# Splitting slot 0's rows and planning the slots before the slot tables, in a fused encoder layer on one core

## The reference

```python
t = rms_norm(h, norm_moe_g).reshape(B * S, D)                 # 1024 rows of 1024
g_prob = softmax(t @ w_group + b_group); g_idx = argmax(g_prob) # 4 groups
e_logits = (t @ w_router + b_router)[group g_idx]             # 4 experts in a group
top_p, top_i = top_k(softmax(e_logits), 2)                    # two experts per row
weights = g_w * top_p / sum(top_p)
for e in range(16):
    he = silu(t @ w_gate[e]) * (t @ w_up[e])                  # 1024 -> 512
    moe = moe + gates[:, e:e + 1] * (he @ w_down[e])          # 512 -> 1024
h = h + moe
```

## Time and profile before

| | us |
|---|---|
| median of 3 runs | 1494.66 |
| their range | 1491.63 to 1494.96 |
| the profiled execution | 1493.72 |
| its span, first to last instruction | 1491.9 |
| PE busy | 1413.1 (95%) |
| DVE busy | 972.7 (65%) |
| ACT busy | 855.9 (57%) |
| POOL busy | 147.1 (10%) |

### The profile page before, as it was taken

One profiled execution on the slowest core, in us unless ns is written; L12 is line 12 of the kernel. 1 busy time (PEld: TensorE's weight loads), 2 busy tenths in 40 slices (PEclk: granted clock), 3 DMA queues, 4 the chain that ended last, 5 costly groups with the idle time before them and its releaser, 6 DMA issues.

```text
span 1491.9 us, 21096 instructions
## 1 busy us (share of the span) xinstructions
PE 1413.1 (95%) x7429; PEld 1082.8 (73%) x7429; DVE 972.7 (65%) x1763; ACT 855.9 (57%) x1553; POOL 147.1 (10%) x205
## 2 busy tenths in 40 slices
PE   6999999999999989999999999988999999999996
PEld 5888989544445544458878888767788888888885
DVE  5513116367658866767763343378888888989887
ACT  6321457366657656653252333344677887888776
POOL 1000000122300200000000000001111112221221
PEclk9999999999999999999999999997999999999998
DMA  6331134420020001021120001146996666666694
GB/s 226 71 111 35 61 107 155 177 103 1 1 113 1 1 7 51 29 95 47 43 113 29 29 29 57 51 148 247 352 361 201 213 216 211 216 216 217 222 373 133
DMA packets 89396, 189.01 MB, mean 127 GB/s; under 512 B 14313, under 2 KB 24553, under 8 KB 88562
## 3 DMA queue, kind: packets, MB, share of 16 engines
q1 hardware_dynamic: 80050, 166.11, 31.2%
q0 software_dynamic: 7200, 22.03, 5.7%
q10 hardware_dynamic: 2080, 0.01, 0.1%
HBM read 218.54 MB, written 28.31 MB: 165 GB/s over the span
## 4 chain that ended last, share of the span: by engine, by line
PE 71%; DMA 10%; DVE 8%; ACT 6%; issue 4%; POOL 1%; DVEq 0%; ACTq 0%; SPq 0%; POOLq 0%
PE psum L2065 26%; PE psum L2313 17%; DMA up_stage<-in_w_up 8%; PE psum L2049 8%; PE psum L2208 6%; PE psum L2231 4%; PE psum L2190 4%; PE psum L2042 3%; DVE up_rest L1676 3%; DMA down_stage<-in_w_down 1%; DVE gate_rest L1676 1%; PE psum L2475 1%; ACT arena L1363 1%; ACT up_high L1223 1%; ACT arena L1198 1%
## 5 line engine op out<-in xcount | busy, mean ns | idle before, releaser
L893 ACT ACTIVATE arena<-psum 128x512 f32<-128x512 f32 (+3 forms) x195 | 85.7, 494 | 87.0 <-PE psum L2231 50.3
L1676 DVE TENSOR_TENSOR down_rest<-down_stage,down_high 128x1024 fp32r<-128x1024 f32 x96 | 115.1, 1219 | 26.4 <-ACT down_high L1223 26.4
L1676 DVE TENSOR_TENSOR up_rest<-up_stage,up_high 128x1024 fp32r<-128x1024 f32 x100 | 117.1, 1221 | 16.2 <-ACT up_high L1223 16.0
L2208 PE MATMUL psum<-arena 64*128 64x512 f32 (+7 forms) x384 | 114.4, 516 | 11.1 <-ACT arena L1179 8.9
L1561 DVE TENSOR_TENSOR_SCAN arena<-arena,singles 128x768 f32<-128x768 f32 (+7 forms) x64 | 86.4, 1364 | 55.6 <-POOL arena L781 45.9
L2049 PE MATMUL psum<-arena 128*128 128x512 f32 (+2 forms) x352 | 118.0, 487 | 0.8 <-DVE arena L1546 0.8
L1676 DVE TENSOR_TENSOR gate_rest<-gate_stage,gate_high 128x1024 fp32r<-128x1024 f32 x100 | 115.8, 1219 | 2.0 <-ACT gate_high L1223 1.9
L2065 PE MATMUL psum<-up_high,rows_high 128*128 128x256 f32 x384 | 110.4, 287 | 6.9 <-DVE up_rest L1676 6.6
L1223 ACT ACTIVATE up_high<-up_stage 128x1024 fp32r<-128x1024 f32 x100 | 100.3, 1056 | 25.3 <-DMA up_stage<-in_w_up 25.3
L2065 PE MATMUL psum<-up_rest,rows_high 128*128 128x256 f32 x384 | 108.6, 283 | 0.0
L2065 PE MATMUL psum<-up_high,rows_rest 128*128 128x256 f32 x384 | 108.6, 283 | 0.0
(11 more groups left out here) (417 smaller groups left out, 3543.4 us busy)
## 6 DMA issues: line engine op xcount, KB each, us to landing
gate_stage<-in_w_gate SPq DMA_DIRECT2D x25, 2048.0 KB
up_stage<-in_w_up SPq DMA_DIRECT2D x25, 2048.0 KB
down_stage<-in_w_down SPq DMA_DIRECT2D x24, 2048.0 KB
arena<-in_x SPq DMA_DIRECT2D x16, 512.0 KB, 3.7
arena<-in_w_mkv SPq DMA_DIRECT2D x8, 1024.0 KB, 6.4
arena<-in_w_in SPq DMA_DIRECT2D x4, 1024.0 KB, 10.6
arena<-in_w_mo SPq DMA_DIRECT2D x4, 1024.0 KB, 6.6
mv_times_w_mo_spill<-arena SPq DMA_DIRECT2D x8, 512.0 KB, 3.2
```

The costliest lines, as they stand in the source:

```text
L893: do(act.activation(dst, src, ACT.Copy), s_te["act"])
L1676: ins = dve.tensor_tensor(split[part][1][:, k, :], stage[part][:, k, :], split[part][0][:, k, :].bitcast(F32), ALU.subtract)
L2208: mm = pe.matmul(scores_of(kind, n)[:, at:end], lhs, rhs(at, end), start=True, stop=True)
```

## The change

On SP the first load of a down matrix is issued ahead of the last tile's two writes instead of behind them. On ACT the four steps of slot 0's gate `high` stand ahead of the last tile's exponentials. On DVE slot 0's gate `rest` steps stand at other places: 0 ahead of the last tile's `probabilities`, 1 behind them, 2 and 3 where 0 and 1 were; the plan of the slots stands right behind `idx`; each half of the tables is cut in `entries(c)` and `lanes(c)`, and the split of slot 0's rows comes behind `entries(0)`; up `rest` 2 and 3 stand ahead of the shares. On PE slot 0 is written out ahead of the loop, and the 16 table products follow its gate products.

```diff
@@ -709,13 +709,13 @@
                     sp.wait_ge(s_mq, T)
                     load(0, 0)
                     load(0, 1)
+                if j == T - 1:
+                    sp.wait_ge(s_mop, T)
+                    load(0, 2)
                 sp.wait_ge(s_tn, j + 1)
                 sp.dma_start(tn_dram[rows(ORDER[j]), :], tn).then_inc(s_tnd, 16)
                 sp.dma_start(out2[rows(ORDER[j]), :].rearrange("p (a b) -> p a b", a=DC),
                              h2[:, :, rows(ORDER[j])]).then_inc(s_ys, 16)
-            sp.wait_ge(s_mop, T)
-            load(0, 2)
-
             sp.wait_ge(s_plan, 1)
             n_slots = sp.value_load(ends_i[0:1, NE - 1:NE], min_val=NE, max_val=SLOTS - 1)
 
@@ -1298,15 +1298,14 @@
 
             act.wait_ge(s_t, ROUND[("router", T - 3, 0)] + 1)
             wide(("mqT", T - 1), mqT)
+            high(0, 0, None)
             exponentials(T - 1, mp_last)
             act.wait_ge(s_mop, T - 1)
             wide(("pT", T - 1), mpT[0], s_mph)
             act.wait_ge(s_h2, T - 1)
             mean_square_of(T - 2, m2[:, 0:1], s_h2q)
             wide(("tT", T - 2), tT)
-            high(0, 0, None, (0, 1))
             strips_copied(T - 2)
-            high(0, 0, None, (2, 3))
 
             def last_squares(half):
                 act.wait_ge(s_h2, T + half)
@@ -1887,11 +1886,13 @@
             do(dve.tensor_copy(before_r, before[:, :]))
             do(dve.tensor_copy(marks[:, T, :], tiny[:, 0:1].to_broadcast([P, NE])))
             do(dve.memset(ends_0[:, 0:1], 0.0))
+            rest(0, 0, (0,))
             probabilities(T - 1, mp_last)
+            rest(0, 0, (1,))
             h2_made(T - 2)
             turned_rest(("pT", T - 1), mpT, s_mph, T - 1)
             moe_input(T - 2)
-            rest(0, 0, (0, 1))
+            rest(0, 0, (2, 3))
             logits(T - 2)
             do.settle()
             group_choice(T - 2)
@@ -1913,7 +1914,6 @@
                                      moe_g[:, 512 * half:512 * half + 512].rearrange("p (a b) -> p a b", a=4), ALU.mult), s_hg)
 
             last_h2(0)
-            rest(0, 0, (2,))
             last_h2(1)
             dve.wait_ge(s_h2q, T + 1)
             one(dve.tensor_scalar(m2[:, :], m2_last[:, 0:1], m2_last[:, 1:2], EPS, ALU.add, ALU.add))
@@ -1954,6 +1954,12 @@
                                          op0=ALU.mult, op1=ALU.add), s_te["dve"])
             dve.wait_ge(s_first, 1)
             do(dve.tensor_scalar(idx[:, 0:1], bank(4)[:, 0:1], -1.0, 0.0, ALU.add, ALU.max), s_idx0)
+            dve.wait_ge(s_ys, FIRST_ROWS)
+            one(dve.tensor_tensor(slot_cmp, slotf[:, :].unsqueeze(2).to_broadcast([P, SLOTS, NE]), along(ends, SLOTS), ALU.is_ge))
+            one(dve.tensor_reduce(expert_of, slot_cmp, AX.X, ALU.add))
+            one(dve.tensor_scalar(expert_of, expert_of, float(NE - 1), None, ALU.min))
+            do(dve.tensor_copy(eidt[:, :], expert_of))
+            one(dve.tensor_tensor(newt[:, 1:SLOTS], expert_of[:, 1:SLOTS], expert_of[:, 0:SLOTS - 1], ALU.not_equal), s_plan)
             one(dve.tensor_tensor(picked.rearrange("p (c t) e -> p c t e", c=2), mark.rearrange("p (c t) e -> p c t e", c=2),
                                   place.unsqueeze(1).to_broadcast([P, 2, T, NE]), ALU.mult))
             flat = posk[:, :, :].rearrange("p c t -> p (c t)")
@@ -1962,17 +1968,18 @@
             do(dve.tensor_scalar(adr[:, 0, :], flat, P - 1, None, ALU.bitwise_and))
             one(dve.tensor_scalar(adr[:, 1, :], flat, 7, None, ALU.logical_shift_right))
             one(dve.tensor_copy(adrf[:, :, :], adr[:, :, :]))
-            rest(0, 0, (3,))
             dve.wait_ge(s_tnd, 16 * T)
-            dve.wait_ge(s_ys, FIRST_ROWS)
             hit = junk[:, 0:2 * T * TAB].rearrange("p (c s) -> p c s", c=2 * T)
-            for c in range(2):
+
+            def entries(c):
                 v = slice(c * T, c * T + T)
                 one(dve.tensor_tensor(hit[:, v, :], slot_no.unsqueeze(1).to_broadcast([P, T, TAB]),
                                       adrf[:, 1, v].unsqueeze(2).to_broadcast([P, T, TAB]), ALU.is_equal))
                 for i, factor in enumerate((tok1[:, :], share_high[:, v].bitcast(F32), share_rest[:, v])):
                     do(dve.tensor_tensor(table_at[:, v, i, :], hit[:, v, :], factor.unsqueeze(2).to_broadcast([P, T, TAB]),
                                          ALU.mult))
+
+            def lanes(c):
                 for v in (slice(c * T, c * T + T // 2), slice(c * T + T // 2, c * T + T)):
                     do(dve.tensor_tensor(onehot[:, v, :], lane.unsqueeze(1).to_broadcast([P, T // 2, P]),
                                          adrf[:, 0, v].unsqueeze(2).to_broadcast([P, T // 2, P]), ALU.is_equal), s_ab)
@@ -1984,12 +1991,12 @@
                     dve.tensor_tensor(xT[1][:, v, :], bank(half).rearrange("p (a b) -> p a b", a=4),
                                       xT[0][:, v, :].bitcast(F32), ALU.subtract).then_inc(s_xl, 1)
 
+            entries(0)
             rows_rest(0)
-            one(dve.tensor_tensor(slot_cmp, slotf[:, :].unsqueeze(2).to_broadcast([P, SLOTS, NE]), along(ends, SLOTS), ALU.is_ge))
-            one(dve.tensor_reduce(expert_of, slot_cmp, AX.X, ALU.add))
-            one(dve.tensor_scalar(expert_of, expert_of, float(NE - 1), None, ALU.min))
-            do(dve.tensor_copy(eidt[:, :], expert_of))
-            one(dve.tensor_tensor(newt[:, 1:SLOTS], expert_of[:, 1:SLOTS], expert_of[:, 0:SLOTS - 1], ALU.not_equal), s_plan)
+            lanes(0)
+            entries(1)
+            lanes(1)
+            rest(0, 1, (0, 1))
             dve.wait_ge(s_tab, 1)
             found = bank(6)[:, 0:TAB]
             do(dve.tensor_scalar(idx_all[:, :, 0], found, -1.0, 0.0, ALU.add, ALU.max))
@@ -1997,10 +2004,9 @@
             one(dve.tensor_scalar(pads, found[:, 0:SLOTS], 0.0, pad_row[:, 0:1], ALU.is_equal, ALU.mult))
             one(dve.scalar_tensor_tensor(out=idx_all[:, 2:TAB, 1], in0=found[:, 0:SLOTS], scalar=-1.0, in1=pads,
                                          op0=ALU.add, op1=ALU.add), s_idx)
-            rest(0, 1, (0, 1))
+            rest(0, 1, (2, 3))
             one(dve.tensor_copy(share, bank(6)[:, TAB:2 * TAB]))
             one(dve.tensor_tensor(share, share, bank(6)[:, 2 * TAB:3 * TAB], ALU.add))
-            rest(0, 1, (2, 3))
             n_slots = dve.value_load(ends_i[0:1, NE - 1:NE], min_val=NE, max_val=SLOTS - 1)
             with dve.Fori(0, n_slots) as s:
                 for half, full in enumerate((s_ua, s_ub)):
@@ -2480,18 +2486,16 @@
                 pe.wait_ge(s_lo[part], 2 * s + half + 1)
 
             pe.wait_ge(s_te["dve"], EMPTIED[ROUND[("rank", 0, 0)]][1])
-            table(range(T // 2))
             rows_in(0)
-            table(range(T // 2, 2 * T)).then_inc(s_tab, 1)
-            pe.wait_ge(s_ends, 1)
-            n_slots = pe.value_load(ends_i[0:1, NE - 1:NE], min_val=NE, max_val=SLOTS - 1)
-            with pe.Fori(0, n_slots) as s:
+            def slot(s):
                 pe.wait_ge(s_xl, 2 * s + 2)
                 rows = lambda a, k: xT[a][:, k, :]
                 for part in range(2):
                     weights(s, 0, part)
                     split_product(bank(2), DC, rows, lambda b, k: split[0][b][:, k, :], s_gf if part else None,
                                   range(4 * part, 4 * part + 4))
+                if isinstance(s, int):
+                    table(range(2 * T)).then_inc(s_tab, 1)
                 for half, full in enumerate((s_ua, s_ub)):
                     cols = slice(256 * half, 256 * half + 256)
                     for part in range(2):
@@ -2515,6 +2519,12 @@
                                       lambda b, k: split[2][b][:, k, 512 * half:512 * half + 512],
                                       s_y if part else None, range(2 * part, 2 * part + 2))
 
+            slot(0)
+            pe.wait_ge(s_ends, 1)
+            n_slots = pe.value_load(ends_i[0:1, NE - 1:NE], min_val=NE, max_val=SLOTS - 1)
+            with pe.Fori(1, n_slots) as s:
+                slot(s)
+
 
 def prod_count(kind, u):
 
```

## The result

The changed kernel took 1500.39 us as the median of 5 executions (1499.46 to 1502.26), against 1494.96 for five of before (1491.63 to 1495.37): ratio 1.0041, interval 1.0024 to 1.0057. The forecast was 1496.9 with a range to 1500.0, so it missed, by little, on the slow side. Its profiled execution took 1500.52 us, with a span of 1498.7 (before: 1491.9).

The account below looks back on a forecast made before the run. It took the PE and DVE chain at the seam between routing and experts as the bound; four parts shift DVE's second hidden product by +2.2 us, so 1494.66 + 2.2 = 1496.9 us, range 1492.6 to 1500.

Parts of the forecast that it names:

- the sum: Seam between routing and experts: DVE's second product of the hidden values comes at 1036.6 instead of 1034.40, +2.2 us.
- Theory Y: Set up for the follow-ups: something outside the seam between routing and experts costs over 4 us in every execution.
- Part 1: Last tile: down load issued about 5.5 us earlier, ahead of the last writes, costs 0.
- Part 2: Last tile: slot 0's gate high steps ahead of the exponentials make h2 later by 0.35 us, bounds 0 to 0.9.
- Part 3: Row numbers to slot 0's gate: gate starts at 1019.45 instead of 1020.99, set by the rows' fetch, and takes 7.5 us.
- Part 4: Behind slot 0's gate: late tables make DVE wait 3.6 us, value_load is exposed (+0.85); second hidden product +2.2 us.
- Part 5: Slot plan ahead of tables: slot 1's earlier gate load worth nothing; its fetch beside the up load loses 0 to 0.6.
- B: Rival, slot loop: slot 1's early gate load repays the delay, so no change, 1494.7 us; chance 0.14.
- D: Rival, last tile: two first loads share bandwidth, gate matrix lands only at 978.5, +6.5 in all, 1501.2 us; chance 0.07.
- E: Rival, PE clock: stays half until the tables are done, +4.2 on top of 2.2, 1501.1 us; chance 0.06.
- C: Rival, slot 0's gate: full clock at once (5.5 us), rows land at 1015.1, value_load hidden, 1.9 earlier, 1492.8 us; chance 0.11.
- The last sign: Slot loop: forecast is wrong if the loop from the second hidden product to the end changes length.

Follow-up runs that it names:

- the early split alone: Kernel before, with only slot 0's gate high steps ahead of the exponentials and its four rests in earlier gaps; median 1494.14 us, ratio 0.9986.
- the up rests first: Changed kernel with all four up rests ahead of DVE's wait for the tables; median 1499.95 us, ratio 1.0038.
- slot 0 written out: Kernel before with only PE's slot 0 written out ahead of its loop, table products still ahead of the gate; ratio 1.0003.

## Why the prediction was wrong

**The step that failed is the last one, "I predict 1494.66 + 2.2 = 1496.9", with its range of -4.3 and +3.1.** It took the median of three executions as the kernel's own time and built the range from the rivals alone, with no spread for the executions to come. The 120 executions of before lie between 1489.2 and 1503.4, mean 1495.1, standard deviation 3.0; medians of three drawn from them scatter by 2.0, medians of five by 1.6. The miss of 3.5 us (1500.4 against 1496.9) consists of 0.4 from the three executions that I started from (1495.1 against 1494.66), 0.7 from the sum (2.9 against 2.2), and 2.4 from the five executions measured (1500.4 against 1498.0, the mean over all 29 of the changed kernel). The last is 1.5 times the scatter of such a median, no rare event. Both scatters together are 2.6. To hold eight times in ten, a range needs 1.28 times that, 3.3 us to either side, for the scatter alone, and more for the doubt in the sum; the range reached 3.1 upwards, and all of that was given to the doubt in the sum. The spread was to be seen: three executions of before were 3.3 us apart.

**Theory Y fell.** The difference shrank from 5.4 to 2.9 us (1.6 to 4.1) over 29 executions, which the seam explains (+2.0 to +3.6 in three profiles). The mean granted clock doesn't speak for a systematic loss ahead of the seam either: 0.9842 over the 29, 0.9833 over 115 of before. The half clock around the routing is 3.4 us shorter in the profiles of the changed kernel (20.5 us instead of 23.9), which accounts for the 0.001. And not every execution of it can have started late: six of the 29 took 1494.8 us or less. If such an execution needs the 526.9 us from the gate load to the end that the first profile has, the shortest of the three, its gate load went out by 966.1 (an estimate). One thing speaks the other way: all three profiles of the changed kernel have the gate load at 970 or later, while of the eleven others only two have it at 969 or later (one is the early split alone, which is not slow) and nine at 964.1 to 965.8, five of which hold most of the change. By the upper bound of 4.1, less the seam's 2.3 at up load 2, up to 1.8 us could arise there; that isn't excluded.

**Point by point.**
- Part 1, down load ahead, 0: no wait on it is seen. Right as far as the profile shows.
- Part 2, +0.35: measured +0.04, +0.46 and +0.02 at h2 in the three profiles, so the term was too big in two of them. The gate was there first, 8.37 us behind its issue, while gate and up loads were both queued. The Trainium skill (DMA: Bandwidth & Descriptors, Queues, rings and completion order) doesn't promise this order; here the loads kept it.
- Part 3, the gate 1.54 sooner, set by the fetch: measured 1.6 to 1.8 in the first profile, 1.3 to 1.9 over the three. The gate's length, 7.5 taken: 7.15, 8.47, 8.22. The mis-sized term is the clock's return, 4.3 us behind the first gate product: it was 3.1, 5.8 and 5.3, and each microsecond of it costs half of one. The gate's mean of 7.95 for 7.5 and the 1.15 below for 0.85 are most of why the seam is +2.8 on average instead of +2.2.
- Part 4: tables 1.74 (1.6 forecast), DVE's wait 2.77, 4.08 and 3.82 (3.6), value_load and what follows 1.15 (0.85), PE standing 1.58 in the up products (1.5). The mechanism is confirmed by undoing it (+0.5 left), and by the up rests first (some 2.3 us sooner with a like clock).
- Part 5, plan ahead worth nothing: right for the gate of the changed kernel, wrong for the loop. Behind the up rests it costs 2.5 us at up load 2 against the second profile of the change (0.4 of it at the hidden product, where its clock was back later). That slot 1's fetch beside the up load loses 0 to 0.6 was right for the changed kernel, where no wait for it is seen: it goes out 2.2 us ahead of that load, and the gate load has long gone. With the up load 2.8 us ahead of it, or a gate load 1.2 ahead, PE waits 2.5 and 2.0 us.
- The rivals: B fell (the bounds of +2.9, 1.6 to 4.1, leave out zero), D fell (landing at 8.37), E fell (the clock was back within the gate). C's condition didn't hold by itself. Forced, it gave the gate what C said, 5.74 us for 5.5, but the second hidden product came 0.2 us earlier than before, not 1.9: C also had the rows landed earliest and the count's load hidden.
- The last sign, a loop of the same length, held in the three profiles of the change (443.3 to 443.6 us from up load 2 to the end; two profiles of before have 444.4 and 443.0). That one profile can be 6 us longer there, as with slot 0 written out, no forecast had.
